# A hybrid recurrent decoder step on one core: the samples' state step moved into the chunk stages, a two-operation state update, and GpSimd held back as a layer opens

## What is computed

```python
sa = einsum('bhk,bhkv->bhv', at, S)
S = wt[..., None] * S + bt[..., None] * sa[:, :, None, :] + kt[..., None] * vt[:, :, None, :]
o = einsum('bhk,bhkv->bhv', rt, S)
```

## Time and profile before

| | us |
|---|---|
| median of 3 runs (lowest, highest) | 2609.24 (2609.24, 2613.75) |
| the profiled execution | 2608.05 |
| its span, first to last instruction | 2606.3 |
| TensorE busy | 2329.2 |
| VectorE busy | 1144.6 |
| GpSimd busy | 875.6 |
| ScalarE busy | 675.8 |
| mean granted TensorE clock | 0.947 of full speed |

### The profile page before, as it was taken

One profiled execution on the slowest core, in us unless ns is written; L12 is line 12 of the kernel. 1 busy time (PEld: TensorE's weight loads), 2 busy tenths in 40 slices (PEclk: granted clock), 3 DMA queues, 4 the chain that ended last, 5 costly groups with the idle time before them and its releaser, 6 DMA issues. The chain is left out here.

```text
span 2606.3 us, 46548 instructions
## 1 busy us (share of the span) xinstructions
PE 2329.2 (89%) x20608; PEld 2150.6 (83%) x20608; DVE 1144.6 (44%) x1558; ACT 675.8 (26%) x867; POOL 875.6 (34%) x620
## 2 busy tenths in 40 slices
PE   5988987788899989999989889777898999999997
PEld 3877876688778989999978789666887799999997
DVE  5165465565444532221143557655636455222212
ACT  2332221311213232222223332103112233222221
POOL 2322310143223434444443133102423334444442
PEclk8999987889999999999989999878899999999998
DMA  7331121111223323322233311211112322222222
GB/s 259 122 115 67 58 71 65 42 46 47 93 89 107 125 91 118 122 90 90 90 125 115 122 60 62 79 45 42 53 54 79 131 99 81 90 91 96 84 96 74
DMA packets 68456, 233.38 MB, mean 90 GB/s; under 512 B 10784, under 2 KB 11296, under 8 KB 67872
## 3 DMA queue, kind: packets, MB, share of 16 engines
q1 hardware_dynamic: 61344, 214.88, 24.0%
q10 hardware_dynamic: 6912, 15.53, 1.6%
HBM read 219.03 MB, written 11.35 MB: 88 GB/s over the span
## 5 line engine op out<-in xcount | busy, mean ns | idle before, releaser
L742 POOL TENSOR_TENSOR ring_lo<-ring,w_hi 128x512 fp32r<-128x512 f32 x552 | 764.7, 1406 | 1302.7 <-ACT w_hi L1376 1277.1
L810 PE MATMUL gm<-H_hi,ring_lo 128*128 128x260 f32 x3456 | 739.1, 295 | 59.0 <-POOL ring_lo L742 23.5
L810 PE MATMUL gm<-H_hi,w_hi 128*128 128x260 f32 x3456 | 712.9, 288 | 2.9 <-issue 2.9
L810 PE MATMUL gm<-H_lo,w_hi 128*128 128x260 f32 x3456 | 711.3, 288 | 0.0
L810 PEld LDWEIGHTS gm<-H_hi,ring_lo 128*128 128x128 f32 x3456 | 549.9, 193 | 97.4 <-DVE H_lo L1810 21.9
L810 PEld LDWEIGHTS gm<-H_hi,w_hi 128*128 128x128 f32 x3456 | 545.2, 193 | 4.3 <-issue 3.5
L810 PEld LDWEIGHTS gm<-H_lo,w_hi 128*128 128x128 f32 x3456 | 545.0, 193 | 0.9 <-issue 0.5
L1376 ACT ACTIVATE w_hi<-ring 128x1024 fp32r<-128x1024 f32 x250 | 264.1, 1056 | 450.5 <-PE gm L810 189.7
L1291 PE MATMUL gm<-AF_hi,ring_lo 128*128 128x260 f32 x704 | 142.2, 283 | 3.3 <-DVE AF_lo L2355 3.3
L759 POOL TENSOR_TENSOR X<-X,GT 128x520 f32<-128x520 f32 x32 | 48.9, 1527 | 282.5 <-DVE GT L2331 282.5
L1291 PE MATMUL gm<-AF_hi,w_hi 128*128 128x260 f32 x704 | 141.7, 282 | 0.0
(11 more groups left out here) (389 smaller groups left out, 2752.2 us busy)
## 6 DMA issues: line engine op xcount, KB each, us to landing
ring<-wall SPq DMA_DIRECT2D x372, 512.0 KB, 3.2
WB<-wbranch SPq DMA_DIRECT2D x32, 256.0 KB, 3.6
xsave<-X SPq DMA_DIRECT2D x2, 2080.0 KB, 12.1
X<-xsave ACTq DMA_DIRECT2D x8, 520.0 KB, 5.1
arena<-states ACTq DMA_DIRECT2D x8, 512.0 KB, 3.2
sst<-arena ACTq DMA_DIRECT2D x8, 512.0 KB, 3.6
X<-xt SPq DMA_DIRECT2D x1, 2080.0 KB, 12.1
y<-H SPq DMA_DIRECT2D x4, 520.0 KB, 2.7
```

The source lines that it names most:

```text
L742: pool.tensor_tensor(ring_lo[:, SLOT[i], k], ring[:, SLOT[i], k], hi[:, k].bitcast(F32), ALU.subtract).then_inc(parts_ready, 1)
L810: ins = pe.matmul(out[:, hf, 0:HALF], w[a][:, k, :], src[b][:, k, HALF * hf:HALF * (hf + 1)], start=first and a == "lo", stop=last and a == b)
```

## The change

1. The two sample stages of each mixer are gone. Their VectorE operations are steps of a generator `decode`; `beside_chunk` takes one step ahead of each wait in the chunk stages, in RWKV and DeltaNet from chunk 2 on (one step earlier in the inverse), in the others in all four. The sample sums get banks 2 and 3 of `mx` for themselves, the chunk's products banks 0 and 1; `SD`, `TA`, `TB` get SBUF that the chunks of that mixer don't use. TensorE makes the sums at fixed places in the chunks (`sample_sums`). The loading of RWKV's and DeltaNet's states moves ahead of the inverse. `AT_SAMPLES` and its filler are gone, `AFTER` has two stages and some weight fewer per mixer.
2. The state update: the product of state and decay (in RWKV the mask times a decay) is made into `KEPT` ahead of the wait; behind it one operation takes the product and one makes the state. RWKV's state is carried already scaled, in `SM` and `SN` in turn, with the scaling in `EC`.
3. As a layer opens, GpSimd waits after tile 0 until seven tiles of `H_lo` are made; its memset and the small weights come ahead of tile 4. ScalarE makes the high parts of tiles 0 and 1 within the norm, after its tiles 1 and 5.
4. DeltaNet's and RWKV's inverse take convolution steps, too. DeltaNet's start waits for RWKV's stores.

```diff
 AT_BANK = {("ada", 0, 18): 18, ("proj", 1, 2): 18, ("proj", 2, 0): 12}
-AT_SAMPLES = {0: (8, 0), 1: (22, 5), 2: (0, 5), 3: (0, 0)}
...
         GD: [4, 4, 3, 3, 4, 4], RT: [3, 3, 3]}
-AFTER = {HG: [8, 4, 4, 4], RW: [8, 4, 4, 4, 4], GD: [8, 4, 4, 4], RT: [8, 4, 4, 4]}
+AFTER = {HG: [6, 4], RW: [6, 4, 4], GD: [6, 4], RT: [6, 4]}
 IDLE = {n: BEFORE[n] + 2 * PAIR[n] + AFTER[n] for n in range(4)}
...
+        RHS, U = GRF[:, 1024:1280], GRF[:, 1280:1536]
+        ST, KEPT = (GRF[:, a:a + 256].rearrange("p (t i) -> p t i", t=2) for a in (1536, 1792))
...
+        LOW = rows(GRF[:, 0:1024])
+        SD = {HG: LOW, RW: slot(1), GD: slot(1), RT: LOW}
+        TA = {HG: rows(SCF[:, 2048:3072]), RW: LOW, GD: LOW, RT: rows(SCF[:, 1024:2048])}
+        TB = {HG: rows(SCF[:, 3072:4096]), RW: slot(7), GD: slot(7), RT: rows(SCF[:, 2048:3072])}
+        SQ = {HG: WK[:, 1], GD: WK[:, 4], RT: WK[:, 1]}
         ROPE = WK[:, 5]
...
+                         and (j < 2 or j >= mixing + 2 and j - mixing - KT not in (0, 1)
                               or (2 <= j < mixing + 2 and room_after[i] <= at[j - 2]))}
             rounds_after = {at[j - 2]: j in on_scalar for j in range(2, mixing + 2)}
...
-                first_tiles = 2
-                for j in range(first_tiles):
-                    split(j)
...
-                                   ).then_inc(beta_split, 1)
...
+                                       ).then_inc(beta_split, 1)
+                for j in range(len(splits)):
+                    if j == 1:
+                        pool.wait_ge(operands_v, KT - 1)
+                    if j == 4:
+                        split_small()
+                        pool.memset(SCF[:, 0:2048], 0.0).then_inc(scores_zeroed, 1)
                     for jx in range(max(0, j - 2), j):
...
+                def sample_sums(x, parts=(0, 1)):
+                    if 0 in parts:
+                        pe.wait_ge(sample_ready, count.next(sample_ready))
+                    for k in parts:
+                        ins = pe.matmul(mx[:, 2 + k, :], cst("blocks"), x[:, 8 * k:8 * k + 8, :].rearrange("p b v -> p (b v)"),
+                                        start=True, stop=True)
+                    if 1 in parts:
+                        ins.then_inc(sample_made, 1)
...
                         ins.then_inc(mix_done_v, 1)
+                        if c == 2:
+                            sample_sums(TB[n], (0,))
...
-                            ins = pe.matmul(mx[:, 1, f:f + HD], MT[:, u, :], RHS[:, f:f + HD], start=True, stop=True)
+                            ins = pe.matmul(mx[:, 0, 256 + f:256 + f + HD], MT[:, u, :], RHS[:, f:f + HD], start=True, stop=True)
                         ins.then_inc(mix_done_v, 1)
+                        if c == 2:
+                            sample_sums(TB[n], (1,))
                         operands(FILL_CHUNK)
...
+                        o = mx[:, 0, P128 * t:P128 * (t + 1)]
                         if n != GD:
...
+                            o = mx[HD * e:HD * (e + 1), 1, P128 * t:P128 * (t + 1)]
                             if n != GD:
...
+                    if c == 0 and not solved:
+                        sample_sums(TB[n])
+                    if c == 2 or c == 3 and solved:
+                        sample_sums(TA[n])
...
+                def norm(sh, rounds=()):
...
                         step(act.activation(H_hi[:, k, 0:SEQ], H[:, k, 0:SEQ], ACT.Identity,
                                             bias=MOD[:, sh + k, 0:1]), for_vector)
+                        if k in rounds:
+                            round_weights()
...
-                def samples(n):
+                def stored_states(n):
                     step(act.activation(mark[:, :], cst("one")[0:4], ACT.Copy), for_vector)
...
                     act.wait_ge(store_ready, n + 1)
...
-                        yield from inverse()
                         if cp:
                             load_states(RW)
+                        yield
+                        yield from inverse()
                         for ci in range(2):
...
+                norm(0, (1, 5))
...
+                        beside()
+                    else:
+                        next(samples[0], None)
                 def early():
                     dve.wait_ge(evac[0], (g[0] + 1) // 2)
...
+                    beside()
                     products()
                     for a in (0, 2 * BLK):
...
+                        next(samples[0])
                     products()
                     top, low = slice(0, 2 * BLK), slice(2 * BLK, 4 * BLK)
-                    step(ts(MT[top, :, low], mx[top, 0, :].rearrange("p (u i) -> p u i", u=8), -1.0, None, MUL),
-                         operands_v if n == GD else vector_step)
...
+                    masked = two_heads.unsqueeze(1).to_broadcast([P128, 2, P128])
+                    x = mx[:, 0, 0:256].rearrange("p (t i) -> p t i", t=2)
                     if n == RW:
-                        for t in range(2):
-                            step(ts((SM, SN)[c % 2][:, t, :], S[:, t, :], EM[:, t, c:c + 1], None, MUL),
-                                 (vector_step, operands_v)[t])
-                        now, then = S, S
+                        now, then = ((SM, SN), (SN, SM))[c % 2]
+                        then = S if c == NC - 1 else then
                     else:
                         now, then = ((S, SM), (SM, S))[c % 2]
+                    now, then = now[:, :, :], then[:, :, :]
                     if n in (RW, GD):
-                        beside()
+                        beside_chunk(n, c)
                         products()
                         if n == RW:
                             step(ts(RHS, mx[:, 0, 0:256], -1.0, None, MUL), operands_v)
                         else:
                             step(tt(RHS, TK[:, 0, c].rearrange("p t i -> p (t i)"), mx[:, 0, 0:256], SUB), operands_v)
-                        beside()
+                        beside_chunk(n, c)
                         products()
-                        step(dve.tensor_copy(U, mx[:, 1, 0:256]), operands_v)
-                    beside()
+                        step(dve.tensor_copy(U, mx[:, 0, 256:512]), operands_v)
+                    if n == RW:
+                        step(tt(KEPT, masked, per_chunk(EC, c), MUL))
+                    else:
+                        step(tt(KEPT, now, per_chunk(CD, c), MUL))
+                    beside_chunk(n, c)
                     products()
-                    x = mx[:, 3, 0:256].rearrange("p (t i) -> p t i", t=2)
                     if n == RW:
-                        for t in range(2):
-                            (issue, step)[t](stt(ST[:, t, :], x[:, t, :], EC[:, t, c:c + 1], two_heads, MUL, MUL))
+                        step(tt(ST, x, now, ADD))
                     else:
-                        step(tt(ST, x, two_heads.unsqueeze(1).to_broadcast([P128, 2, P128]), MUL))
-                    sem = operands_v if c == 1 or (c == 0 and n != RW) or (c == 2 and n != RW) else vector_step
-                    issue(stt(then[:, 0, :], now[:, 0, :], CD[:, 0, c:c + 1], ST[:, 0, :], MUL, ADD))
-                    step(stt(then[:, 1, :], now[:, 1, :], CD[:, 1, c:c + 1], ST[:, 1, :], MUL, ADD),
-                         sem)
-                def samples(n, out):
-                    from_scalar()
-                    dve.wait_ge(state_loaded, 16 * (n + 1))
-                    if n in (RW, GD):
...
+                    if n not in (RW, GD):
+                        dve.wait_ge(state_loaded, 16 * (n + 1))
+                        step(tt(TB[n], i64b, dib(3), MUL), sample_ready)
+                        step(tt(SD[n], SD[n], dib(0), MUL))
+                        yield
+                        yield
+                        dve.wait_ge(sample_made, count.next(sample_made))
+                        step(tt(TB[n], dec2, dib(2), MUL))
+                        yield
+                        step(tt(SD[n], SD[n], TB[n], ADD))
+                        step(tt(TA[n], SD[n], dib(1), MUL), sample_ready)
+                        yield
+                    else:
+                        step(tt(TB[n], i64b, dib(3), MUL), sample_ready)
+                        yield
+                        dve.wait_ge(state_loaded, 16 * (n + 1))
+                        step(tt(TA[n], SD[n], dib(4), MUL))
+                        yield
+                        step(tt(SD[n], SD[n], dib(0), MUL))
+                        yield
+                        dve.wait_ge(sample_made, count.next(sample_made))
+                        step(tt(TB[n], dec2, dib(2), MUL), sample_ready)
+                        yield
+                        step(tt(SD[n], SD[n], TB[n], ADD))
+                        yield
+                        dve.wait_ge(sample_made, count.next(sample_made))
+                        step(tt(TA[n], dec2, dib(5), MUL))
+                        yield
+                        step(tt(SD[n], SD[n], TA[n], ADD))
```

(26 more changed lines are left out.)

134 lines of the change are left out of this document (56 added, 78 removed).

## The result

| | before | after |
|---|---|---|
| median (lowest, highest) of four, us | 2609.24 (2607.05, 2613.75) | 2515.22 (2513.72, 2519.55) |
| profiled execution; its span | 2608.05; 2606.3 | 2513.72; 2511.9 |
| mean granted TensorE clock | 0.947 | 0.964 |

A forecast was written before the change was run, and what follows sets the result against it. TensorE's own work (busy 2329 of 2606.3 us) plus its waits was taken as the bound; 24.5 + 2.6 + 5.9 - 4.5 = 28.5 us a layer, 57.0 in all, took 2608.05 to 2551.0, forecast 2552, range 2516 to 2588.

The forecast's parts named there:

- Left out of the sum: Large products dealt out anew, one RWKV gate's product sliding into the inverse stages: taken as 0, bounds -5 and +12 a layer.
- Rival 2: The clock stays up in RWKV and waits are filled: 12 us a layer more gain, 2528 us; chance 0.18.
- 1 us at the norm behind the last chunk: Output norm after a mixer's last chunk comes late, under 12 + 30 large matmuls: 1 us for each of two mixers.
- Samples, removed and added: Sample stages' waits, filler and slow clock removed, 24.5 us a layer; their VectorE operations in chunk slots added, 4.5 a layer.
- State update: Two operations between product and state, no RWKV scaling before the chunk, shorter HGRN2 wait: 2.6 us a layer, bounds 0 and 3.
- Opening: Opening norm of a layer, first product ending at 60.4 instead of 66.3: 5.9 us a layer, bounds 3 and 8.
- Rivals 3 to 6: Less gain or loss: 2576, new waits (0.23); 2597, only the opening gains (0.05); 2609, even (0.04); 2627, slots bare (0.05).
- rival 3: Half the samples' gain returns as waits at norms after last chunks and at banks: 12 less a layer, 2576; chance 0.23.
- the two layers repeat each other within some 0.2 us: Both layers taken as alike within some 0.2 us, so one layer was worked and doubled.

The follow-up runs named there:

- third run: Changed kernel with RWKV's weights set so its large products stand where they stood before the change (first weight 16 for 6): 2544.39 us, ratio 0.9748.
- seventh: Changed kernel with HGRN2's large products put back where they stood before the change (first weight 16 for 6): 2524.86 us, ratio 0.9663.
- fourth run: Kernel before, sample stages kept, with RWKV's weights set so its large products stand where the changed kernel has them: 2609.35 us, ratio 1.001.
- fifth run: Changed kernel with the old state update, three operations in place of two, and RWKV's scaling in front of a chunk: 2513.44 us, ratio 0.9623.
- first run: Kernel before with only the opening of the changed kernel: 2599.03 us, ratio 0.9955.
- ninth run: Changed kernel with RWKV's products back in their old places, plus 16, 8, 16 and 8 filler matmuls ahead of the inverse's waits: 2547.44 us, ratio 0.9761.
- thirteenth: Changed kernel with RWKV's products in their old places, plus filler cut to 6, 3, 7 and 2 matmuls ahead of the inverse's waits: 2530.73 us, ratio 0.9705.
- sixteenth: Changed kernel with 48 in place of 18 filler matmuls meant for HGRN2's new bank wait, placed ahead of the wrong product: 2533.15 us, ratio 0.9712.

## Why the prediction was wrong

**The step that failed** is "Left out of the sum": "Bounds -5 and +12 a layer; I take 0, having no row of either". The redistribution of large products gave 28 to 29 us in RWKV (third run) and 6 to 9.6 in HGRN2 (seventh), with 0 to 5 in the two others: 34 to 44 in all, about what the forecast was short by (37). This adds up single edits; no run put all mixers' products back at once. In RWKV alone it is 14.6 us a layer by the medians, above my upper bound, and HGRN2 had no bound at all. The rows were there: the earlier trace rows has one of the inverse's waits and the earlier trace rows the clock of 0.57. I had also written the plan's shift down, but as one gate's product with two signs, where the plan printed before and after shows twelve large products that move in RWKV. It should have been priced: products set into a stretch whose steps wait some 5 us a pair fill these waits, and the same stretch then runs at full clock. Rival 2 had this mechanism and a gain of 12 a layer in RWKV; its 2528 is nearest to the result. It didn't have the norm's wait.

**A term that was right by luck.** The forecast charges 1 us at the norm behind the last chunk for each of two mixers, because 42 large matmuls stand there. With the old places and no sample stages the norm waits 5.9 and 6.3 us in RWKV (third run) and 3.3 and 3.5 in HGRN2 (seventh), and in RWKV the product behind it runs at half clock. Only the redistribution, which I had at nothing, took these waits away.

**Samples, removed and added**: 24.5 - 4.5 a layer, 40.0 in all. What is left of 94 after the opening (12 to 15) and the redistribution (34 to 44) is 35 to 48; the term stands, but by subtraction, not by a run of its own, and only in this order: without the removal the same places gained nothing (fourth run), so the places' share is one that both parts earn together. In RWKV it can be read: 9.7 and 8.2 in the third run's stretches, some 5.5 more for the large product that came in, and the norm's waits of 5.9 and 6.3 already taken off, where the terms for samples and update come to 11.8. The distribution over the mixers was off: the slots are largely covered in the solved mixers as the earlier trace rows suggested, and bare in retention, which gained nothing where 3.3 was in the sum: a wait of 2.40 us and a sample product of 3.58 stand there now. I carried DeltaNet's idle VectorE over to retention without a row of retention's.

**State update**: 2.6 a layer; it measured 0 (fifth run). I had priced the waits of 1.60 and 1.33 in the earlier trace rows as if all behind them came earlier by as much; with the old update back, HGRN2 keeps its length (117.2 / 116.7) and RWKV has 235.5 / 232.8, 3.4 us more over both layers than in after, in an execution 9 us slower than its median.

**Opening**: 5.9 a layer; 5.9 by the first run, 6.4 and 5.6 by the traces' first copies (17.65 and 18.41 after the start, where 24.10 and 24.04 stood). Four of the seven tile intervals are 1.57 to 1.58 us, two are 2.5, and the copy starts at 59.49 for the 60.4 of the forecast; that bears out its steps. Here rows for each term existed.

**Rivals 3 to 6** needed waits at the norms after the last chunks or bare slots in the solved mixers. In after neither has the size they needed: the chunk's waits are 0.6 us at most in the rows above, and of the norms only DeltaNet's waits, 1.8 us as before. The third and seventh runs show that rival 3's wait at the norm was near.

The forecast says that the two layers repeat each other within some 0.2 us. Of the stretches HGRN2 and retention don't (131.5 and 126.9, 215.2 and 209.6 before), which is part of why small differences of stretches say little.

## What to carry to other kernels

When a change shortens a plan by which other work is dealt out, print where each piece of that work falls before and after, and price the move like any other part: here it was worth over a third of the gain, and a few products one stage off lost 15 to 32 us again. A norm or copy that follows directly on a removed stage needed such a product ahead of it here. Filler must be cut to the wait it covers and stand ahead of the wait's own instruction; too much of it gained nothing here (ninth run), and ahead of another product it cost 18 us (sixteenth). And check each mixer's own idle rows before saying that a slot is covered.

## What the runs showed that I had not expected

The granted clock and the time don't go together by themselves: RWKV ran at 0.96 and 248 us (ninth run), at 0.94 and 240 (thirteenth), at 0.97 and 229 (after). The kernel before with filler has a mean clock of 0.951 to 0.957 where 0.944 to 0.948 stood, and the same median. A clock raised by filler is worth what the real matmuls behind it save, less the filler that sticks out.

Filler took 0.12 us a record at full clock, so 0.24 for a matmul of 128 columns in fp32, as two records.
